# A block solver of 64x64 products on TensorE: all products of one corner of the array in a row, then those of the other

## The reference, cut to what matters

```python
def step(state, inp):
    r_t, w_t, k_t, v_t, a_t, b_t = inp
    sa = jnp.einsum('bhvk,bhk->bhv', state, a_t)
    state = state * w_t[:, :, None, :] + sa[..., None] * b_t[:, :, None, :] + v_t[..., None] * k_t[:, :, None, :]
    return state, jnp.einsum('bhvk,bhk->bhv', state, r_t)
_, y = lax.scan(step, state0, xs)
```

## Time and profile before

| | us |
|---|---|
| median of 3 runs | 1202.96 |
| the profiled execution | 1202.91 |
| its span, first to last instruction | 1201.1 |
| TensorE busy | 1157.1 (96%) |
| TensorE weight loads | 1068.1 (89%) |
| VectorE busy | 796.5 (66%) |
| ScalarE busy | 558.7 (47%) |
| mean granted TensorE clock | 0.983 of 2.4 GHz |

### The profile page before, as it was taken

One profiled execution on the slowest core, in us unless ns is written; L12 is line 12 of the kernel. 1 busy time (PEld: TensorE's weight loads), 2 busy tenths in 40 slices (PEclk: granted clock), 3 DMA queues, 4 the chain that ended last, 5 costly groups with the idle time before them and its releaser, 6 DMA issues.

```text
span 1201.1 us, 27163 instructions
## 1 busy us (share of the span) xinstructions
PE 1157.1 (96%) x10708; PEld 1068.1 (89%) x10708; DVE 796.5 (66%) x1452; ACT 558.7 (47%) x963; POOL 1.7 (0%) x10
## 2 busy tenths in 40 slices
PE   7999999999988999999999999999999889999998
PEld 6899998999967799999989999989998678999997
DVE  4666666878634876666686666677885458666665
ACT  4444444675323544444454444456833334444443
POOL 0000000000000000000000000000000000000000
PEclk8999999999997999999999999999999979999999
DMA  6666666644000366666646666665520014666664
GB/s 183 193 182 185 188 182 175 166 124 124 4 2 1 106 192 179 189 184 183 189 142 190 180 191 179 188 172 156 141 73 4 2 35 124 193 189 182 188 184 131
DMA packets 243958, 173.41 MB, mean 144 GB/s; under 512 B 14428, under 2 KB 228596, under 8 KB 243892
## 3 DMA queue, kind: packets, MB, share of 16 engines
q1 hardware_dynamic: 243892, 172.46, 49.6%
HBM read 171.39 MB, written 1.05 MB: 144 GB/s over the span
## 4 chain that ended last, share of the span: by engine, by line
PE 84%; DVE 9%; ACT 5%; issue 2%; DMA 1%; SPq 0%; DVEq 0%; ACTq 0%
PE bank L1327 23%; PE bank L1328 23%; PE bank L1329 23%; PE bank L1340 8%; DVE wlo L798 2%; PE bank L1334 2%; DVE xlo L827 1%; ACT whi L527 1%; PE bank L1364 1%; PE bank L1462 1%; DMA raw<-in_ffn_w_gate_dram 1%; ACT work L635 0%; PE bank L1704 0%; PE bank L1461 0%; PE bank L1706 0%
## 5 line engine op out<-in xcount | busy, mean ns | idle before, releaser
L798 DVE TENSOR_TENSOR wlo<-raw,whi 128x1024 fp32r<-128x1024 f32 (+1 forms) x322 | 391.9, 1221 | 251.2 <-ACT whi L527 250.2
L1327 PE MATMUL bank<-xhi,whi 128*128 128x256 f32 x1696 | 484.1, 285 | 6.6 <-DVE xlo L827 5.8
L1328 PE MATMUL bank<-xlo,whi 128*128 128x256 f32 x1696 | 480.4, 283 | 0.0
L1329 PE MATMUL bank<-xhi,wlo 128*128 128x256 f32 x1696 | 480.4, 283 | 0.0
L527 ACT ACTIVATE whi<-raw 128x1024 fp32r<-128x1024 f32 (+1 forms) x322 | 338.4, 1053 | 294.1 <-PE bank L1329 269.3
L1327 PEld LDWEIGHTS bank<-xhi,whi 128*128 128x128 f32 x1696 | 325.6, 192 | 13.7 <-issue 7.9
L1328 PEld LDWEIGHTS bank<-xlo,whi 128*128 128x128 f32 x1696 | 325.7, 192 | 3.7 <-issue 0.5
L1329 PEld LDWEIGHTS bank<-xhi,wlo 128*128 128x128 f32 x1696 | 325.6, 192 | 0.0
L1327 PE MATMUL bank<-whi,hhi 128*128 128x512 f32 x352 | 138.7, 394 | 6.8 <-DVE hlo L916 6.8
L1328 PE MATMUL bank<-wlo,hhi 128*128 128x512 f32 x352 | 138.0, 392 | 0.0
L1329 PE MATMUL bank<-whi,hlo 128*128 128x512 f32 x352 | 137.0, 389 | 0.0
(11 more groups left out here) (220 smaller groups left out, 1040.3 us busy)
## 6 DMA issues: line engine op xcount, KB each, us to landing
raw<-in_ffn_w_gate_dram SPq DMA_DIRECT2D x88, 512.0 KB, 3.9
raw<-in_ffn_w_up_dram SPq DMA_DIRECT2D x88, 512.0 KB, 3.9
raw<-in_ffn_w_down_dram SPq DMA_DIRECT2D x88, 512.0 KB, 3.5
raw<-in_w_in_dram SPq DMA_DIRECT2D x32, 512.0 KB, 3.9
raw<-in_w_out_dram SPq DMA_DIRECT2D x16, 512.0 KB, 3.6
raw<-in_w_q_up_dram SPq DMA_DIRECT2D x4, 384.0 KB, 3.3
xtok<-in_x_dram SPq DMA_DIRECT2D x4, 256.0 KB, 5.5
raw<-in_w_in_dram SPq DMA_DIRECT2D x4, 256.0 KB, 4.3
```

What stands on the lines that cost most here:

```text
L798: V_.tensor_tensor(wlo[:, b.slot, 0:width], raw[:, b.slot, 0:width], whi[:, b.slot, 0:width].bitcast(F32), ALU.subtract).then_inc(lo_ready, 1)
L1327: mm(out, hi, mhi, start=start, stop=False, **kw)
L1328: mm(out, hi, mlo, start=False, stop=False, **kw)
L1329: return mm(out, lo, mhi, start=False, stop=stop, **kw)
```

## The change

A new helper `by_quarter` takes a list of products and issues the LO half of all of them, then the UP half of all. The groups `u`, `t`, `p`, `br`, `tb`, `tk` and `tv` go through it, with the same products, operands, banks, waits and increments. `gk`, `gl`, the Q turns, the groups `gb` and `ti` ahead of the solver, and the chunk steps keep `both` or are untouched.

```diff
+            def by_quarter(pairs, start, stop, **kw):
+                for half in (LO, UP):
+                    for out, lhs, rhs in pairs:
+                        ins = mm(out[half], lhs[half], rhs[half], start=start, stop=stop, **kw)
+                return ins
...
-                            for j in range(8):
-                                ins = both(out[:, 64 * j:64 * (j + 1)], bC[:, 8 * b + j, :], AR[:, 8 * b + j, 1, :],
-                                           True, True)
+                            ins = by_quarter([(out[:, 64 * j:64 * (j + 1)], bC[:, 8 * b + j, :], AR[:, 8 * b + j, 1, :])
+                                              for j in range(8)], True, True)
...
-                                ins = both(out[:, 64 * j:64 * (j + 1)], src, eyes, True, True)
+                                pairs.append((out[:, 64 * j:64 * (j + 1)], src, eyes))
+                            ins = by_quarter(pairs, True, True)
...
-                        for j in range(8):
-                            g = 8 * b + j
-                            ins = both(bank[4 + b][:, 64 * j:64 * (j + 1)], M1[:, g, 0, :], tC[:, g, :], True, True)
+                        ins = by_quarter([(bank[4 + b][:, 64 * j:64 * (j + 1)], M1[:, 8 * b + j, 0, :], tC[:, 8 * b + j, :])
+                                          for j in range(8)], True, True)
...
-                            for j in range(8):
-                                g = 8 * b + j
-                                ins = both(bank[b][:, 64 * j:64 * (j + 1)], pC[:, g, :], uC[:, g, :], False,
-                                           k == LEVELS - 1, skip_group_check=True)
+                            ins = by_quarter([(bank[b][:, 64 * j:64 * (j + 1)], pC[:, 8 * b + j, :], uC[:, 8 * b + j, :])
+                                              for j in range(8)], False, k == LEVELS - 1, skip_group_check=True)
...
-                        for j in range(8):
-                            g = 8 * b + j
-                            ins = both(bank[2 + b][:, 64 * j:64 * (j + 1)], uC[:, g, :], pC[:, g, :], False, last,
-                                       skip_group_check=True)
+                        ins = by_quarter([(bank[2 + b][:, 64 * j:64 * (j + 1)], uC[:, 8 * b + j, :], pC[:, 8 * b + j, :])
+                                          for j in range(8)], False, last, skip_group_check=True)
```

More of the change, by code:

```diff
@@ L1586, in fill @@
                                 pe.wait_ge(mix_dve.sem, mix_dve.at(l, "sh_v3"))
+                            pairs = []
                             for j in range(8):
```

## The result

The changed kernel takes 1245.05 us (median of 4 runs, 1243.94 to 1245.45) against 1202.86 us before: the medians differ by 42 us. The prediction said 1254, range 1226 to 1274. The profiled execution's span is 1243.7 us against 1201.1, +42.6.

The account below looks back on a forecast made before the run. TensorE's pace was taken to bound the solver. Groups +50.4, ends of chains +0.9 and hidden time at the solver's end -0.5 gave +50.8 us: 1202.9 to 1253.7 us, 4.2% slower, range 1226 to 1274.

Parts of the forecast that it names:

- The bound: In the solver TensorE's pace sets the time, so what a group costs more there ends up in the kernel's time.
- The step of 58.3 ns and two corners at once: In the solver's products, one record takes 58.3 ns in its corner, and both corners work side by side.
- Two records overlap at each change of corner: In the 72 groups: 28 steps in place of 16, +0.700 us a group, +50.4 us.
- The bound with four shared steps: In the 72 groups: three records passed, four steps shared at each change, +0.467 us a group, +33.6 us.
- The rule of program order: TensorE's matmuls stay in program order: LO's last and UP's first share one step, 30 steps a group, +58.8 us.
- Ends of a chain: Ahead of Q0 to Q3 an upper row loses 2 steps, 0.117 us, four times a layer: +0.9 us.
- The end of the solver: From p5_1 to the scores, part of the group's growth is hidden: 0.26 us a layer, -0.5 us.
- "Cost nothing" elsewhere: Copies, masks and waits outside the changed groups cost nothing, and no cover is lost.
- Whole rows passed: Rival: UP's row of 16 starts under LO's, nothing is lost, 1203 us within 1 us; chance 0.13.
- Loads no longer hidden: Rival: neighbours in the same rows of the array expose each weight load, +191 us, 1394 us; chance 0.02.
- The clock: Rival: with one corner at work TensorE's clock falls to 1.2 GHz in the solver, 1372 us; chance 0.02.
- the prediction's last remark: The steps at half clock after the solver may fall differently, moving the sum a few us in either direction.

Follow-up runs that it names:

- the fills alone: Only tb, tv, br and tk in rows of 8, u, t and p through `both`, against the kernel before: 1209.03 us, ratio 1.0071.
- the lower corner alone: The changed kernel without the upper half of the 72 changed groups, timed against the kernel before: 1202.36 us, ratio 1.0001.
- rows of 8: The changed kernel itself, corners changing after every 8 products, against the kernel before: 1245.05 us, ratio 1.0365.
- rows of 3: The changed kernel with corners changing after every 3 products, timed against the kernel before: 1203.52 us, ratio 1.0013.
- rows of 4: The changed kernel with corners changing after every 4 products, timed against the kernel before: 1218.67 us, ratio 1.0126.

## Why the prediction was right, step by step

- **The bound** held. All of the loss but 0.9 us lies in the two solver stretches, and with the fills alone it scales with the number of groups.
- **The step of 58.3 ns and two corners at once** held, and the lower corner alone confirms it.
- **"Two records overlap at each change of corner"** is the term that was mis-sized. Three do, by the timeline, by the saved 0.179 us at rows of 8 and of 4, and by the pace of rows of 3. A group costs 0.575 us more, not 0.700: 72 groups 41.4 us, not 50.4. The earlier trace rows show one waiting record passed because the order of issue there offers no more; I read the least that the row shows as the size. The bound with four shared steps was as near, and its mechanism is the one in the trace: three records are passed, and what it lacks are the 54 ns a change. It gives +33.6 us, and 144 x 0.054 = 7.8 more make 41.4.
- **The rule of program order.** The Trainium skill ("TensorE: Matmul & The Clock Gate", Part 2) keeps matmuls in program order; by it the loss would have been 58.8 us. The trace of the changed kernel differs: a matmul of the next row starts ahead of three that stand before it in the program (305.88 against 305.94 to 306.05).
- **Ends of a chain.** A group behind a full-width piece shares nothing at its start: in the chain of layer 0, t4_0 with p4_0 take 3.33 us against 2.01 before, +1.32, which is 2 x 0.575 and 0.17, and the piece with p5_0 takes 1.82 against 1.08, +0.74, which is 0.575 and 0.17. So each such end costs three steps, 0.17 us, not two: 8 x 0.17 = +1.4 us where +0.9 was said. The first group of each solver, behind `both`, starts its row alone too, which the prediction left out (some +0.3, worked out as 2 x 0.17).
- **The end of the solver.** From p5_1's start to the scores it is 2.59 us (349.37 to 351.96) against 1.95, +0.64 where the group grew by 0.575 + 0.17: 0.11 a layer hidden, not 0.26. The group ended nearly where it was forecast: ScalarE's last copy starts 1.94 us after p5_1's start, forecast 1.97. It was the copy that was mis-sized. From its start to the scores it is 0.65 us (0.60 of copy and 0.05 behind it), where half of the two copies' 1.07, 0.54, was put.
- **"Cost nothing" elsewhere** was near. The terms so far make 41.4 + 1.4 + 0.3 - 0.2 = 42.9, and the two stretches grew by 41.7. The 1.2 us between them are small gaps of TensorE before; one of them the chain of layer 1 shows as 0.30 us of issue at 886.71, and none such stands in the chain after. Which wait each of the others was is not shown.
- **Whole rows passed**, 1203 us: no. The reach is three waiting records, not fourteen. The Trainium skill (same page, head table) gives the queue 64 entries; a matmul doesn't pass that far here, the rows of 4 already lose.
- **Loads no longer hidden**, 1394 us: no. In a row of one corner the records come 58.3 ns apart, loads included, where this rival had 112. That stands against the rule of the Trainium skill (same page, Part 3) that loads overlap only matmuls of other rows.
- **The clock** stood at 1.00 through both solvers.

Summed up: 50.8 - 9.0 (groups) + 0.8 (ends) + 0.3 (end of the solver) - 1.2 (gaps) + 0.9 outside the solver, where nothing was worked out, gives the 42.6 us of the span. The 0.9 are a sum of both signs: up to the first stretch 0.2 us shorter, between the stretches 0.4 shorter, and behind the second 1.5 longer (277.8 to 279.3 us). In the 77.78 us behind the second, TensorE's mean granted clock is 0.89 where it was 0.91, and in the 68.93 us behind the first 0.90 where it was 0.88. This fits the prediction's last remark, on the steps at half clock; that the clock is the cause was not tested.

No version here is faster than the kernel before. With the corners in turn each corner already works at its own pace of 58.3 ns a record (lower corner only), so the order of these groups has nothing left to win.

## What to carry to other kernels

Small products in two corners of the array run side by side only if their instructions stand close together: rows of up to 3 products (6 float32 records) per corner kept the pace, 4 cost 0.22 us a group of 16 products, 8 cost 0.575. Even a row of 3 costs 0.16 us wherever full-width work follows, so corners in turn are the safe order. A busy share near 100% says nothing about it; read the pace from the starts, and compare it with what one corner alone must take. And a row that shows an effect shows its least size: when the pattern of issue offers no more, put the range, not the point, on that row.

## What the runs showed of the hardware

- A 64x64 float32 product is two records; a corner takes one record in 58.3 ns, load included, whether the other corner works or not (ratio 1.0001 with the upper half left out).
- A matmul passes matmuls issued before it, if they wait for the other corner: the first of a new row starts ahead of the last three of the old one (305.88 against 305.94 to 306.05). Each change of corner saves 0.179 us, 3.07 steps, with 64 moving columns and 0.38 us, 3.5 steps, with 128: in both cases four steps less some 55 ns.
- The two corners write the same bank, on different partitions, side by side: 32 records of both in 0.933 us, the time that 16 of one corner take alone.
- With one corner alone at work in 20 of the 26 steps of a group the granted clock stayed at 1.00 for 63 us (287.85 to 351.30), and with the lower corner alone in the changed groups for 43 us (1.00, 288 to 331).
